# The odd layer's key and value weights at the end of the first expert stage, and routed rows read and added in quarters of a tile

## The chip, the cores and the metric

The kernel runs on one core of a Trainium2 chip. The metric is the device time of one execution in microseconds. The core has TensorE (PE: matrix products, with PEld its weight loads), VectorE (DVE), ScalarE (ACT), GpSimd (POOL) and SyncE (SP), which here only issues DMAs and clears semaphores. Engines run their own instruction lists and wait on semaphores. Sixteen DMA engines are shared by all queues; DMAs from SyncE go through one hardware queue, those of GpSimd through a software queue.

## The reference

A two-layer backbone over 256 context tokens and 256 latent tokens, width 1024, all in float32. Layer 0 mixes with neighbourhood and grouped-query attention, layer 1 with differential attention. Behind each mixer comes a mixture of experts: 64 experts of width 256, each token goes to 8 of them. What matters here is the step between the two layers:

```python
y = moe_ffn(tokens, *moe_args)            # layer 0, 512 tokens: sum over 8 routed experts + shared expert
xc = xc + g_fc * y[:, :L]                 # context
x = x + g_f * y[:, L:]                    # latent
...
h = modulate(rms_norm(x, norm_mix[l]), sh_m, sc_m)      # layer 1
q, k, v = jnp.split(hs @ w_in, 3, axis=-1)              # diff_mixer: w_in is 1024 x 3072
```

## The kernel before, in words

Tokens lie in four tiles of 128 rows: tiles 0 and 1 the context, 2 and 3 the latents. The program is a sequence of stages; at the end of each, all engines meet in a block end, then SyncE clears the stage's semaphores one by one (L245), then all meet again.

Stage `ffn0` (`feed_forward`) computes the routed experts in R rounds of 128 slots. In a round, GpSimd gathers token rows (L1355), TensorE transposes them (L1418), multiplies by gate and up weights (L1448), ScalarE and VectorE form the hidden rows (L1456, L1462), TensorE transposes them (L1470) and multiplies by the down weights (L1492), VectorE and ScalarE scale the result by the token's gate (L1529, L1538), and GpSimd scatters it to `y_rows` in HBM (L1363). `y_rows` holds, for each token, its 8 expert rows. Gate and up weights of an expert take one of four slots of `wb` (`wgu`, two 1 MB halves each), the down weights one of five other slots, two of them in `hT`. SyncE loads them in the order of the experts and waits, before it fills a slot, until TensorE has used it for the last time. After the last scatter GpSimd waits for both scatter semaphores (L1721). Then `further` reads a counter that says whether an expert got more rows than planned; only in that case does a slow fallback run (`fb_sp` and others). It isn't taken with these inputs.

The same four slots of `wb` also serve `Stream`, a list of weight blocks of 512 columns (2 MB) which SyncE feeds with `core.stream.feed` and TensorE takes with `core.stream.take`. Block n goes to slot n % 4. The first four blocks of the odd layer's projection, `diff_w_kv`, hold the keys' and values' columns; their first block has number 31 and goes to slot 3.

Stage `mix1` (`combine_project`) reads the eight rows of each token back, adds them up, gates the sum and adds it to the residual `x`, takes the norm, transposes, modulates, and projects to keys, values and (for the latents) queries. SyncE reads the rows of a tile in two halves of four rows (L2054). VectorE waits for a half and adds (L2104 to L2109), multiplies with the gate (L2111), adds to `x` (L2112). ScalarE squares and sums (L2150) and takes the root (L2153), VectorE inverts and scales (L2114 to L2118), TensorE transposes (L2075), VectorE and ScalarE modulate half of the transposed tile each (L2123, L2159), and TensorE multiplies (L2092): 4 blocks for each of 4 tiles, then 2 query blocks for tiles 2 and 3, 40 products of 8 matmuls. TensorE transposes tile t+1 ahead of the last block of tile t.

Of the kernel before, what the change touches and what calls it, by code (L numbers as in the profile page):

```python
# [16 lines left out]
ALU = mybir.AluOpType  # L17
ACT = mybir.ActivationFunctionType
AX = mybir.AxisListType.X

P = 128
D = 1024
# [14 lines left out]
E = 64  # L37
TOP_K = 8
F = D // 4
# [4 lines left out]
TILES = (CTX + LAT) // P  # L44
# [218 lines left out]
STREAM = 4  # L263
# [869 lines left out]
def feed_forward(core, r, sw, final_norm):  # L1133
# [15 lines left out]
    last = r.out is not None  # L1149
    XS = RING - 1 if last else RING  # L1150
    with Stage(nc, f"ffn{layer}") as st:
# [45 lines left out]
        if last:  # L1197
# [3 lines left out]
            gain = core.pool[:, 3, D:2 * D]  # L1201
# [8 lines left out]
        r.slots = wgu  # L1210
        wd = [core.pool[:, 0, :], core.pool[:, 1, :], core.hT[:, 0:4, :].rearrange("p k t -> p (k t)"),
# [369 lines left out]
        def fb_sp(sp, b, e, n):  # L1581
            sp.wait_ge(fb_free, n + 1)
            for dst, src in ((wgu[0][:, 0, :], r.gate_src), (wgu[0][:, 1, :], r.up_src), (wd[0], r.down_src)):
                sp.dma_start(dst, r.of(src, e)).then_inc(fb_w_in, 16)
# [62 lines left out]
        def fb_pe(pe, b, e, n):  # L1647
# [11 lines left out]
            w = wgu[0].rearrange("p i (k f) -> p k i f", f=F)  # L1659
# [23 lines left out]
        with nc.Block() as block:  # L1683
            @block.sync
            def _(sp):
# [8 lines left out]
                for q in range(E - LAG, E):  # L1694
                    sp_down(sp, q)
                if last:
                    sp.wait_ge(xb_turned, R)
                    sp.dma_start(gain, final_norm.rearrange("(o d) -> o d", o=1).to_broadcast([P, D])).then_inc(gain_in, 16)
# [315 lines left out]
def combine_project(core, r, w):  # L2014


    nc = core.nc
    COLS = BLOCK
    HALF = TOP_K // 2
    first = core.stream.start["diff_w_kv"]  # L2020
    kv = 2 * D // COLS
    with Stage(nc, "mix1") as st:
        yr = st.sb("yr", [P, 2, HALF, D])
# [3 lines left out]
        y_in = [st.sem("y_in0"), st.sem("y_in1")]  # L2027
# [19 lines left out]
        with nc.Block() as block:  # L2047
            @block.sync
            def _(sp):
                def rows(n):  # L2050
                    if n >= 2:

                        sp.wait_ge(y_used, n - 1)
                    sp.dma_start(yr[:, n % 2], y_view[n // 2][:, HALF * (n % 2):HALF * (n % 2 + 1), :]).then_inc(y_in[n % 2], 16)  # L2054

                rows(0)
                rows(1)
                core.stream.feed(sp, first + 1, first)
                rows(2)
                core.stream.feed(sp, first + 2, first)  # L2060
                rows(3)
                core.stream.feed(sp, first + kv, first)
                for n in range(4, 2 * TILES):
                    rows(n)
                core.stream.feed(sp, core.stream.end["diff_w_out"], first, lambda b: (summed, last_use(b)))
# [31 lines left out]
            def _(dve):  # L2097
                link = Chain(dve, own)
                for t in range(TILES):
                    acc = xn[:, t, :]  # L2100
                    for half in range(2):
                        dve.wait_ge(y_in[half], 16 * (t + 1))
                        v = yr[:, half]
                        link(nc.vector.tensor_tensor(v[:, 0:2], v[:, 0:2], v[:, 2:4], ALU.add))  # L2104
                        if half == 0:
                            nc.vector.tensor_tensor(acc, v[:, 0], v[:, 1], ALU.add).then_inc(y_used, 1)
                        else:
                            link(nc.vector.tensor_tensor(acc, acc, v[:, 0], ALU.add))
                            nc.vector.tensor_tensor(acc, acc, v[:, 1], ALU.add).then_inc(y_used, 1)  # L2109
                        dve.wait_ge(y_used, 2 * t + half + 1)  # L2110
                    link(nc.vector.tensor_tensor(acc, acc, grow[:, t // 2, :], ALU.mult))  # L2111
# [35 lines left out]
            def _(act):  # L2147
# [13 lines left out]

                square(0)
# [325 lines left out]
```

## Time and profile before

| what | value |
|---|---|
| three runs | 1970.25, 1970.87, 1976.96 us; median 1970.87 |
| profiled execution | 1975.1 us, span 1973.3 us |
| TensorE busy | 1739.5 us, 88% of the span |
| VectorE, ScalarE, GpSimd busy | 568.7, 312.3, 207.1 us |
| DMA | 560.50 MB, mean 284 GB/s over the span |
| mean granted TensorE clock | 0.956 |

A profile is one execution. Busy times are those of the engines' instructions; waits are read between them. A clock of 1.0 is the upper of TensorE's two levels (2.4 GHz), 0.50 the lower (1.2 GHz). The span is not made of one limit: in the expert stages the weights stream at about 390 GB/s and TensorE is nearly full, in the stages between, short chains over all engines count.

### The profile page before, as it was taken

Reading aid. Unit: us, or ns where it says so; the run is one execution under the profiler, and the core shown is the slowest. Engines: PE = TensorE matmul, PEld = TensorE weight load, DVE = VectorE, ACT = ScalarE, POOL = GpSimd, SP = SyncE. Lnnn points to the kernel's source line nnn. Section 1 sums busy time; section 2 is a strip of 40 time slices with the busy share of each in tenths; the row PEclk is TensorE's granted clock in tenths of the full one; section 3 lists DMA queues with packets and bytes.
Section 4 is the critical chain, followed back from the end, with each engine's and each line's share of the span. In section 5 each row is a group of like instructions: output and inputs, shape, how many; then the busy total and the mean of one; then the engine's idle time right before and its main releaser. Section 6 shows DMA issues by size and latency. Waiting matters only on the chain. (4 is left out here: it accounts for less than half of the span.)

```text
span 1973.3 us, 23640 instructions
## 1 busy us (share of the span) xinstructions
PE 1739.5 (88%) x8663; PEld 793.9 (40%) x8663; DVE 568.7 (29%) x1345; ACT 312.3 (16%) x686; POOL 207.1 (10%) x197
## 2 busy tenths in 40 slices
PE   4999999998999999999998199888779989988895
PEld 2544544446443334333433044354423333333231
DVE  2131445435422222212221343275321111111112
ACT  2102333212011111111111011062201011001011
POOL 0300222100111111111111000020010000000000
PEclk8999999997999999999999599989889999999998
DMA  9414667005699999999997570400499999999992
GB/s 355 120 64 143 229 225 243 14 0 192 269 418 399 409 419 395 416 418 402 418 412 321 228 287 25 146 5 0 158 420 407 407 420 396 420 419 419 419 406 98
DMA packets 125188, 560.50 MB, mean 284 GB/s; under 512 B 17266, under 2 KB 22785, under 8 KB 74896
## 3 DMA queue, kind: packets, MB, share of 16 engines
q1 hardware_dynamic: 106960, 512.20, 65.0%
q0 software_dynamic: 17248, 43.62, 5.8%
q10 hardware_dynamic: 864, 3.15, 0.4%
q8 instruction: 71, 1.16, 0.2%
q14 instruction: 45, 0.37, 0.1%
HBM read 549.94 MB, written 26.80 MB: 292 GB/s over the span
## 5 line engine op out<-in xcount | busy, mean ns | idle before, releaser
L1448 PE MATMUL ps<-wb,pool 128*32 128x512 f32 (+2 forms) x2608 | 486.7, 600 | 19.3 <-issue 19.3
L1448 PEld LDWEIGHTS ps<-wb,pool 128*32 128x32 f32 (+2 forms) x2608 | 159.8, 124 | 306.6 <-issue 306.5
L1462 DVE TENSOR_TENSOR ffn_hid<-ffn_sg,ps 128x256 f32<-128x256 f32 x71 | 29.9, 422 | 607.9 <-ACT ffn_sg L1456 607.9
L1492 PE MATMUL ps<-pool,ffn_hidT 128*32 128x512 f32 (+2 forms) x584 | 165.9, 604 | 23.9 <-DVE ffn_hidT L1477 10.8
L1492 PE MATMUL ps<-hT,ffn_hidT 128*32 128x512 f32 (+2 forms) x680 | 157.7, 599 | 19.7 <-DVE ffn_hidT L1477 14.8
L1355 POOL DMA_INDIRECT pool<-h_rows,ffn_index x71 | 74.6, 1051 | 655.9 <-PE ps L1418 306.5
L2092 PE MATMUL ps<-wb,hT 128*128 128x512 f32 x320 | 140.8, 602 | 1.6 <-issue 1.6
L1456 ACT ACTIVATE ffn_sg<-ps 128x256 f32<-128x256 f32 x71 | 27.2, 383 | 489.1 <-PE ps L1448 489.1
L1492 PE MATMUL ps<-sh_wd,ffn_hidT 128*32 128x512 f32 (+2 forms) x272 | 100.3, 597 | 4.6 <-DVE ffn_hidT L1477 2.6
L1418 PEld LDWEIGHTS ps<-const,pool 128*128 128x128 f32 x568 | 77.5, 194 | 66.6 <-issue 63.3
L1510 PE MATMUL ps<-x_res,rw 128*128 128x512 f32 x224 | 103.1, 603 | 0.9 <-ACT x_res L1538 0.9
L1418 PE MATMUL ps<-const,pool 128*128 128x128 f32 x568 | 94.1, 289 | 8.3 <-DMA pool<-h_rows,ffn_index 6.2
L1363 POOL DMA_INDIRECT y_rows<-sh_wgu,ffn_index x43 | 43.1, 1002 | 486.5 <-ACT sh_wgu L1538 472.0
L2092 PEld LDWEIGHTS ps<-wb,hT 128*128 128x128 f32 x320 | 61.6, 194 | 78.2 <-issue 78.2
L1433 ACT COPY pool<-ps 128x512 f32<-128x512 f32 x71 | 41.6, 585 | 296.5 <-PE ps L1418 296.5
L985 PE MATMUL ps<-wb,hT 128*128 128x512 f32 x192 | 83.4, 593 | 3.4 <-PEq L241 3.4
L1448 PE MATMUL ps<-ffn_wgu_more,pool 128*32 128x512 f32 (+1 forms) x208 | 73.9, 622 | 5.7 <-issue 5.7
L948 POOL TENSOR_SCALAR attn_pn<-attn_p,attn_mx 128x256 f32<-128x256 f32 (+1 forms) x43 | 53.1, 1235 | 241.3 <-DVE attn_mx L886 239.7
L1426 DVE COPY pool<-ps 128x512 f32<-128x512 f32 x71 | 48.8, 688 | 90.3 <-PE ps L1418 89.9
L1448 PE MATMUL ps<-sh_wgu,pool 128*32 128x512 f32 (+2 forms) x256 | 72.7, 602 | 1.6 <-issue 1.6
L368 PE MATMUL ps<-wb,silu 128*32 128x512 f32 x384 | 54.1, 687 | 22.1 <-DMA wb<-in_ada_w_dram 17.6
L1492 PEld LDWEIGHTS ps<-pool,ffn_hidT 128*32 128x32 f32 (+2 forms) x584 | 45.3, 127 | 69.4 <-issue 62.6
(287 smaller groups left out, 1905.0 us busy)
## 6 DMA issues: line engine op xcount, KB each, us to landing
wb<-in_expert_w_gate_dram SPq DMA_DIRECT2D x108, 1024.0 KB, 12.9
wb<-in_expert_w_up_dram SPq DMA_DIRECT2D x108, 1024.0 KB, 17.8
pool<-in_expert_w_down_dram SPq DMA_DIRECT2D x52, 1024.0 KB, 18.8
hT<-in_expert_w_down_dram SPq DMA_DIRECT2D x52, 1024.0 KB, 17.1
wb<-in_ada_w_dram SPq DMA_DIRECT2D x24, 2048.0 KB, 9.6
sh_wd<-in_expert_w_down_dram SPq DMA_DIRECT2D x24, 1024.0 KB, 19.8
mix_yr<-y_rows SPq DMA_DIRECT2D x8, 2048.0 KB, 11.8
wb<-in_diff_w_in_dram SPq DMA_DIRECT2D x6, 2048.0 KB, 16.8
```

The source lines that it names most:

```text
L368: mm = nc.tensor.matmul(core.ps[g:g + 32, bank, :], core.silu[:, k, :], w[:, k, :], start=k < 4, stop=k >= 4, skip_group_check=True, tile_ ...
L948: nc.gpsimd.tensor_scalar(pn[:, n % 4, 0:nk], p[:, n % 4, 0:nk], mx[:, n % 4, 3:4], None, ALU.mult).then_inc(norm_pool, 1)
L985: mm = nc.tensor.matmul(core.ps[:, n % 6, :], core.hT[:, k, oT_at(t)], wo[:, k, :], start=k == 0, stop=k == KD - 1)
L1355: pool.indirect_dma_start(out=xs[:, s, :], out_offset=None, in_=r.h_rows, in_offset=bass.IndirectOffsetOnAxis(ap=index[:, n, 0:1], axis=0) ...
L1363: pool.indirect_dma_start(out=r.y_rows, out_offset=bass.IndirectOffsetOnAxis(ap=index[:, n, 1:2], axis=0), in_=y[:, n % 2, :], in_offset=N ...
L1418: mm = nc.tensor.transpose(core.ps[:, x_bank(half), (k % 4) * P:(k % 4 + 1) * P], xs[:, s, k:D:KD], core.c("ident"))
L1426: nc.vector.tensor_copy(xT[:, n % 2, 0:4, :].rearrange("p k c -> p (k c)"), core.ps[:, x_bank(0), :]).then_inc(xa_ready, 1)
L1433: nc.scalar.copy(xT[:, n % 2, 4:8, :].rearrange("p k c -> p (k c)"), core.ps[:, x_bank(1), :]).then_inc(xb_ready, 1)
L1448: mm = nc.tensor.matmul(core.ps[lo:lo + width, gu_bank(n), :], xT[:, n % 2, k, lo:lo + width], w[:, k], start=k == 0, stop=k == KD - 1, sk ...
L1492: mm = nc.tensor.matmul(core.ps[lo:lo + width, down_bank(half), :], hidT[:, n % 2, k, lo:lo + width], wd_at(q % DR, half, k), start=k == 0 ...
L1510: mm = nc.tensor.matmul(core.ps[:, 4 + 2 * i + half, :], back_hot[:, n % 2, i * P:(i + 1) * P], y[:, n % 2, half * 512:(half + 1) * 512], ...
L2092: mm = nc.tensor.matmul(core.ps[:, n % 6, :], core.hT[:, k, t * P:(t + 1) * P], wb[:, k, :], start=k == 0, stop=k == KD - 1)
```

## The change

It has five parts.

1. At the end of SyncE's list in `ffn0`, ahead of `further`, the four key and value blocks are fed. Each waits until the last expert that uses its slot has been multiplied. They are no longer fed in `mix1`.
2. The fallback's gate and up weights go to `hT` instead of slot 0 of `wb`, which now holds a key and value block.
3. `mix1` reads a tile in four quarters of two rows: 16 DMAs of 1 MB instead of 8 of 2 MB, with a semaphore and a buffer for each quarter.
4. VectorE adds quarter by quarter. The first three are summed, gated and added to `x`; the last is summed, gated and added to `x` by itself.
5. ScalarE takes one square root of a constant ahead of everything in `mix1`.

```diff
     XS = RING - 1 if last else RING
+    ahead = core.stream.start["diff_w_kv"]
...
+        fb_wgu = core.hT[:].rearrange("p k t -> p (k t)").rearrange("p (i n) -> p i n", i=2)
...
                 for q in range(E - LAG, E):
                     sp_down(sp, q)
+                if not last:
+                    for n in range(ahead, ahead + STREAM):
+
+                        user = max(q for q in range(E) if q % GU == n % STREAM)
+                        sp.wait_ge(gu_ready, plan.last(user) + 1)
+                        core.stream.feed(sp, n + 1, ahead)
...
-                rows(0)
-                rows(1)
-                core.stream.feed(sp, first + 1, first)
...
+                for n in range(PARTS * TILES):
+                    if n >= PARTS:
+
+                        sp.wait_ge(y_used, n - PARTS + 1)
+                    i = n % PARTS
+                    sp.dma_start(yr[:, i], y_view[n // PARTS][:, PART * i:PART * (i + 1), :]).then_inc(y_in[i], 16)
...
-                        if half == 0:
+                    gain = grow[:, t // 2, :]
+                    for i in range(PARTS):
+                        dve.wait_ge(y_in[i], 16 * (t + 1))
+                        v = yr[:, i]
+                        if i == 0:
                             nc.vector.tensor_tensor(acc, v[:, 0], v[:, 1], ALU.add).then_inc(y_used, 1)
+                        elif i < PARTS - 1:
+                            link(nc.vector.tensor_tensor(v[:, 0], v[:, 0], v[:, 1], ALU.add))
+                            nc.vector.tensor_tensor(acc, acc, v[:, 0], ALU.add).then_inc(y_used, 1)
                         else:
...
+                            link(nc.vector.tensor_tensor(acc, acc, gain, ALU.mult))
+                            link(nc.vector.tensor_tensor(core.x[:, t, :], core.x[:, t, :], acc, ALU.add))
+                            link(nc.vector.tensor_tensor(v[:, 0], v[:, 0], v[:, 1], ALU.add))
+                            nc.vector.tensor_tensor(acc, v[:, 0], gain, ALU.mult).then_inc(y_used, 1)
+                        dve.wait_ge(y_used, PARTS * t + i + 1)
                     nc.vector.tensor_tensor(core.x[:, t, :], core.x[:, t, :], acc, ALU.add).then_inc(x_ready, 1)
...
+                nc.scalar.activation(rs[:, 1, 0:1], core.c("ones")[:, 0:1], ACT.Sqrt)
                 square(0)
```

How the instructions stand. On SyncE at the end of `ffn0`, before (L1129, L1130, L1347 load the last expert's weights, L1555 is the read of the counter in `further`):

```order
L1129 DMA wb<-in_expert_w_gate_dram 128x2048
L1130 DMA wb<-in_expert_w_up_dram 128x2048
L1122 TENSOR_LOAD ffn_eid
L1122 ISA x2
L1347 ISA
L1347 DMA hT<-in_expert_w_down_dram 128x2048
L1555 TENSOR_LOAD ffn_longest
L1555 ISA x2
```

and after:

```order
L1129 DMA wb<-in_expert_w_gate_dram 128x2048
L1130 DMA wb<-in_expert_w_up_dram 128x2048
L1122 TENSOR_LOAD ffn_eid
L1122 ISA x2
L1349 ISA
L1349 DMA hT<-in_expert_w_down_dram 128x2048
L295 DMA wb<-in_diff_w_in_dram 128x8x512 x4
L1557 TENSOR_LOAD ffn_longest
L1557 ISA x2
```

The four blocks now stand between the last expert's down weights and the read of the counter. In `mix1`, SyncE before:

```order
L2054 DMA mix_yr<-y_rows 128x4096 x2
L295 DMA wb<-in_diff_w_in_dram 128x8x512
L2054 DMA mix_yr<-y_rows 128x4096
L295 DMA wb<-in_diff_w_in_dram 128x8x512
L2054 DMA mix_yr<-y_rows 128x4096
L295 DMA wb<-in_diff_w_in_dram 128x8x512 x2
L2054 DMA mix_yr<-y_rows 128x4096 x4
L295 DMA wb<-in_diff_w_in_dram 128x8x512 x2
```

and after (with the clears of `ffn0` ahead of it):

```order
L245 ISA x73
L241 UNCONDITIONAL_BRANCH
L2057 UNCONDITIONAL_BRANCH
L2064 DMA mix_yr<-y_rows 128x2048 x16
L295 DMA wb<-in_diff_w_in_dram 128x8x512 x2
L295 DMA wb<-in_diff_w_out_dram 128x8x512 x2
```

Only rows are left ahead of the two query blocks. On VectorE, one tile of `mix1` before:

```order
L2104 TENSOR_TENSOR mix_yr<-mix_yr 128x2048
L2106 TENSOR_TENSOR mix_xn<-mix_yr 128x1024
L2104 TENSOR_TENSOR mix_yr<-mix_yr 128x2048
L2108 TENSOR_TENSOR mix_xn<-mix_xn,mix_yr 128x1024
L2109 TENSOR_TENSOR mix_xn<-mix_xn,mix_yr 128x1024
L2111 TENSOR_TENSOR mix_xn<-mix_xn,ffn_gate 128x1024
L2112 TENSOR_TENSOR x_res<-x_res,mix_xn 128x1024
```

and after (the line numbers are those of the changed file; the wait for the last quarter is on L2111):

```order
L2106 TENSOR_TENSOR mix_xn<-mix_yr 128x1024
L2108 TENSOR_TENSOR mix_yr<-mix_yr 128x1024
L2109 TENSOR_TENSOR mix_xn<-mix_xn,mix_yr 128x1024
L2108 TENSOR_TENSOR mix_yr<-mix_yr 128x1024
L2109 TENSOR_TENSOR mix_xn<-mix_xn,mix_yr 128x1024
L2111 TENSOR_TENSOR mix_xn<-mix_xn,ffn_gate 128x1024
L2112 TENSOR_TENSOR x_res<-x_res,mix_xn 128x1024
L2113 TENSOR_TENSOR mix_yr<-mix_yr 128x1024
L2114 TENSOR_TENSOR mix_xn<-mix_yr,ffn_gate 128x1024
L2116 TENSOR_TENSOR x_res<-x_res,mix_xn 128x1024
```

Seven instructions, two of them twice as wide, have become ten; behind the last wait for rows stand five of 1024 elements where one of 2048 and four of 1024 stood.

## Rows read from the trace of the kernel before

**Rows 1.** The page's first line: span of the profiled execution, and its instructions.

```profile
span 1973.3 us, 23640 instructions
```

**Rows 2.** Windows: us, busy us of each engine (instructions), PEclk, DMA share, GB/s.

```profile
1095.00:1101.50 6.50, 0.00 (x0) 0.00 (x0) 0.00 (x0) 0.00 (x0) 0.00 (x0) 0.50 0.00 0
...
1106.40:1133.50 27.10, 1.97 (x8) 1.59 (x9) 14.22 (x15) 4.14 (x8) 0.00 (x0) 0.50 0.98 387
1133.50:1157.80 24.30, 24.29 (x56) 11.11 (x57) 10.83 (x11) 3.11 (x6) 0.00 (x0) 0.89 1.03 412
1157.80:1276.50 118.70, 118.66 (x290) 53.21 (x288) 40.61 (x54) 14.62 (x31) 0.00 (x0) 1.00 0.30 111
```

**Rows 3.** Timeline: start us, us, engine, line, operation, tiles, [idle before <-releaser].

```profile
1082.99 0.38 ACT L1456 ACTIVATE ffn_sg<-ps 128x256 f32<-128x256 f32 x1 [8.73 <-PE ps L1448]
...
1090.58 0.97 POOL L1363 DMA_INDIRECT y_rows<-sh_wgu,ffn_index  x1 [14.57 <-issue]
...
1106.37 0.82 SPq L2054 DMA_DIRECT2D mix_yr<-y_rows  x2
```

**Rows 4.** L1683 and L245 from 1090 to 1110 us: durations in ns, first and last start.

```profile
L1683 POOLq DRAIN  x1: 7079/7079/7079, 1094.3 to 1094.3; - x1
...
L245 SPq EVENT_SEMAPHORE_RANGE_CLEAR  x73: 25/25/49, 1101.7 to 1106.1; - x73
```

**Rows 5.** Timeline of tile 0 of the stage `mix1`, from the first rows to TensorE.

```profile
1113.84 2.29 DVE L2104 TENSOR_TENSOR mix_yr<-mix_yr 128x2048 f32<-128x2048 f32 x1 [26.01 <-DMA mix_yr<-y_rows]
...
1118.84 2.29 DVE L2104 TENSOR_TENSOR mix_yr<-mix_yr 128x2048 f32<-128x2048 f32 x1 [1.44 <-DMA mix_yr<-y_rows]
1121.16 1.22 DVE L2108 TENSOR_TENSOR mix_xn<-mix_xn,mix_yr 128x1024 f32<-128x1024 f32 x1
...
1124.94 1.22 DVE L2112 TENSOR_TENSOR x_res<-x_res,mix_xn 128x1024 f32<-128x1024 f32 x1
...
1127.36 1.28 ACT L2153 ACT_TABLE_LOAD   x1
1127.38 0.15 DVE L2114 TENSOR_SCALAR mix_rs<-mix_ss 128x1 f32<-128x1 f32 x1 [1.22 <-ACT mix_xn L2150]
1128.65 0.20 ACT L2153 ACTIVATE mix_rs<-mix_rs 128x1 f32<-128x1 f32 x1
...
1129.90 1.97 PE L2075 MATMUL ps<-const,mix_xn 128*128 128x128 f32 x8 [41.14 <-DVE mix_xn L2118]
...
1133.51 23.59 PE L2092 MATMUL ps<-wb,hT 128*128 128x512 f32 x48 [1.64 <-issue]
```

**Rows 6.** Timeline of the same two small steps in tile 1.

```profile
1148.00 0.15 DVE L2114 TENSOR_SCALAR mix_rs<-mix_ss 128x1 f32<-128x1 f32 x1 [1.22 <-ACT mix_xn L2150]
...
1148.19 0.20 ACT L2153 ACTIVATE mix_rs<-mix_rs 128x1 f32<-128x1 f32 x1 [0.22 <-DVE mix_rs L2114]
```

**Rows 7.** Scatters of L1363, issue to landing in us: at 1062.4, at 1090.6, all 43.

```profile
DMA to landing us min/median/max: 9.2/9.2/9.2
...
DMA to landing us min/median/max: 2.6/2.6/2.6
...
DMA to landing us min/median/max: 2.6/8.6/9.6
```

**Rows 8.** Hardware queue from 1062 to 1073 us: packets, MB, share of 16 engines.

```profile
q1 hardware_dynamic: 579, 4.22, 92.0%
```

**Rows 9.** L295: ns of the first four issues; landing of the four, of the first.

```profile
L295 SPq DMA_DIRECT2D wb<-in_diff_w_in_dram x4: 427/1272/6786, 1107.2 to 1126.3; - x4
...
DMA to landing us min/median/max: 16.6/18.7/25.1
...
wb<-in_diff_w_in_dram SPq DMA_DIRECT2D x1, 2048.0 KB, 16.9
```

**Rows 10.** Timeline: rows of tile 2 ready, and the transposes of tile 2.

```profile
1174.03 0.75 DVE L2118 TENSOR_SCALAR mix_xn<-x_res,mix_rs 128x1024 f32<-128x1024 f32 x1
...
1185.28 1.04 PE L2075 MATMUL ps<-const,mix_xn 128*128 128x128 f32 x8
```

More of the change, by code:

```diff
@@ L1582, in fb_sp @@
             sp.wait_ge(fb_free, n + 1)
-            for dst, src in ((wgu[0][:, 0, :], r.gate_src), (wgu[0][:, 1, :], r.up_src), (wd[0], r.down_src)):
+            for dst, src in ((fb_wgu[:, 0, :], r.gate_src), (fb_wgu[:, 1, :], r.up_src), (wd[0], r.down_src)):
                 sp.dma_start(dst, r.of(src, e)).then_inc(fb_w_in, 16)
@@ L1658, in fb_pe @@
             pe.wait_ge(fb_w_in, 48 * n + 48)
-            w = wgu[0].rearrange("p i (k f) -> p k i f", f=F)
+            w = fb_wgu.rearrange("p i (k f) -> p k i f", f=F)
             for k in range(KD):
@@ L2018, in combine_project @@
     COLS = BLOCK
-    HALF = TOP_K // 2
+    PART = 2
+    PARTS = TOP_K // PART
     first = core.stream.start["diff_w_kv"]
@@ L2022, in combine_project @@
     with Stage(nc, "mix1") as st:
-        yr = st.sb("yr", [P, 2, HALF, D])
+        yr = st.sb("yr", [P, PARTS, PART, D])
         grow = r.ffn_gate
         ss, rs = st.sb("ss", [P, TILES]), st.sb("rs", [P, 3, TILES])
-        y_in = [st.sem("y_in0"), st.sem("y_in1")]
+        y_in = [st.sem(f"y_in{i}") for i in range(PARTS)]
         y_used, x_ready, own = st.sem("y_used"), st.sem("x_ready"), st.sem("own")
@@ L2049, in _ @@
             def _(sp):
[L2050 to L2054, printed above, removed]
-                rows(0)
-                rows(1)
-                core.stream.feed(sp, first + 1, first)
[L2059 to L2064, printed above, removed]
+                for n in range(PARTS * TILES):
[3 more added lines that the diff above has]
+                    sp.dma_start(yr[:, i], y_view[n // PARTS][:, PART * i:PART * (i + 1), :]).then_inc(y_in[i], 16)
                 core.stream.feed(sp, core.stream.end["diff_w_out"], first, lambda b: (summed, last_use(b)))
@@ L2100, in _ @@
                     acc = xn[:, t, :]
[L2101 to L2104, printed above, removed]
-                        if half == 0:
+                    gain = grow[:, t // 2, :]
[3 more added lines that the diff above has]
+                        if i == 0:
                             nc.vector.tensor_tensor(acc, v[:, 0], v[:, 1], ALU.add).then_inc(y_used, 1)
-                        else:
[L2108 to L2111, printed above, removed]
+                        elif i < PARTS - 1:
+                            link(nc.vector.tensor_tensor(v[:, 0], v[:, 0], v[:, 1], ALU.add))
+                            nc.vector.tensor_tensor(acc, acc, v[:, 0], ALU.add).then_inc(y_used, 1)
+                        else:
+                            link(nc.vector.tensor_tensor(acc, acc, gain, ALU.mult))
[3 more added lines that the diff above has]
+                        dve.wait_ge(y_used, PARTS * t + i + 1)
                     nc.vector.tensor_tensor(core.x[:, t, :], core.x[:, t, :], acc, ALU.add).then_inc(x_ready, 1)
```

## The prediction, made before the changed kernel ran

> **What bounds the kernel now.** I read the page, then a table of windows around the boundary between the first expert stage (`ffn0`) and the stage that the change touches (`mix1`), then the timeline there, then waits and landings. The profiled execution took 1975.1 us, its span is 1973.3 us [rows 1], and 1.8 us lie around it; the median of the runs is 1970.87 us, 4.2 us below it. The sum is made on the profiled execution and its difference is then taken from the median. From 1133.5 to 1276.5 us TensorE has no hole (24.29 busy of 24.30 us, 118.66 of 118.70) [rows 2]: once `mix1` projects, TensorE bounds it, and no weight block is late. Before that it stands still, from the end of the last down projection to 1129.9 us. So the change can win or lose only in that pause, and what counts is when the first projection begins, 1133.51 us [rows 5].
>
> The pause is one chain. The gate-up product of the last round ends at about 1082.98 (ScalarE starts on it at 1082.99); the last scatter of expert rows is issued at 1090.58 [rows 3] and lands 2.6 us later [rows 7]. GpSimd then leaves the stage through a DRAIN of 7.08 us that begins at 1094.3, and SyncE clears 73 semaphores from 1101.7 to 1106.1 [rows 4]. The first rows are asked for at 1106.37 [rows 3]. The second half of tile 0 is there at 1118.84, 12.47 us later; VectorE needs until 1126.2 to sum and gate it, then come the norm, TensorE's transposes at 1129.90 and the first product at 1133.51 [rows 5]. From 1095 to 1101.5 the DMA engines move nothing, and from 1106.4 on 387 GB/s [rows 2].
>
> **The change, part by part.**
>
> *Weights moved ahead.* Four 2 MB blocks (8.39 MB) now stand at the end of SyncE's list in `ffn0`. The first goes into slot 3, which the last expert uses, so nothing is issued before 1082.98. At 387 GB/s the four take 21.7 us. A 2 MB read of rows lands its 2.10 MB 7.47 us after the issue [rows 3, 5]; 5.4 of these are transfer at that rate, so about 2.1 us are start. The weights are thus done near 1083.0 + 2.1 + 21.7 = 1106.8, and the first rows would begin to arrive only 2.1 us after their issue at 1106.37 or later: no overlap. What is gained by the earlier weights alone is nothing. Block 0 was issued at 1107.24 and landed 16.9 us later [rows 9], at 1124.1, 9.4 us ahead of its first use; rows of tile 0 stand ahead of it in the same queue, so they did not wait for it. The work that hid these loads is VectorE's sum; if that cover were gone, block 0 would still be in time.
>
> Its cost is on the last scatter. That scatter now runs beside 8.39 MB of weights. Alone it lands in 2.6 us; the one issued at 1062.4 beside expert weights took 9.2, and over all 43 the median is 8.6 and the maximum 9.6 [rows 7]. GpSimd waits for this landing, the DRAIN comes after it, SyncE's clears after that, so every microsecond is paid in full. No row shows this scatter beside these blocks, so I bound it: 0 from its own landing alone, +7.0 from the maximum (9.6 - 2.6). Between them I go by packet length. Beside the expert weights the hardware queue moved 4.22 MB in 579 packets [rows 8], 7.3 KB each; a key and value block is 8 x 512 floats a partition, 2 KB pieces. If the delay of 6.6 us (9.2 - 2.6) shrinks with the length of the packet that a scatter's packet must let pass, it is 6.6 x 2.0/7.3 = **+1.8 us**, and this value I take.
>
> The Trainium skill (DMA: Bandwidth & Descriptors, Queues, rings and completion order) speaks against it: a DMA engine takes turns between queues by whole packets of some 9 to 17 descriptors. By that a turn of the weights would be 18 to 34 KB, no less than beside the experts, and the delay would be the whole +6.6. No row here decides it; it is the rival below.
>
> SyncE's four issues: one issue of such a block took between 0.43 and 6.8 us [rows 9], the long ones while earlier blocks were still queued. Two short and two long are 14.5 us from 1083.0, so SyncE reaches the end of the stage near 1097.5, before GpSimd's DRAIN ends at 1101.4 (1094.3 + 7.08) [rows 4]. Cost 0; behind those issues stands only SyncE's branch and barrier. If all four took 6.8 it would be there at 1110.2, 8.8 us late.
>
> *Rows in quarters.* 16 DMAs of 1 MB for 8 of 2 MB, in the same order on the same queue; four reads with nothing between them bring the same 4.19 MB, so the last quarter lands 12.47 us after the first issue, as the second half did. After the landing of the second half VectorE ran one 2048-wide add (2.32 us with the gap: 1118.84 to 1121.16) and four 1024-wide operations, the last of them started at 1124.94 (1.26 us each: (1124.94 - 1121.16)/3) [rows 5], 7.36 us. Now the wait for the last quarter stands before the gating product, so five 1024-wide operations follow it: 5 x 1.26 = 6.30. The third quarter lands some 2.6 us before the last, and its two adds take 2.52, so they are just done. **-1.06 us**. Bounds: -1.1, and 0 if the smaller pieces cost the last quarter a microsecond. Over a tile VectorE's work grows from 10.9 (2 x 2.32 + 5 x 1.26) to 12.6 us. For tiles 1 to 3 that lies under TensorE: rows of tile 2 were ready at 1174.8 and the transposes ran at 1185.28, 10.5 us later [rows 10]. Cost 0, and still 0 if the cover shrank by 8 us. The rows of tiles 1 to 3 wait on VectorE's use of the same quarter one tile before; the weights no longer share the queue with them. Nothing there is late.
>
> *Square root ahead.* The table load (1.28 us at 1127.36) moves to the stage's beginning, where ScalarE idles some 20 us. VectorE's step ends at 1127.53 and the root begins at 1128.65, 1.12 us [rows 5]; in tile 1, without a load, 1148.15 to 1148.19, 0.04 us [rows 6]. **-1.08 us**, bounds -1.3 and 0 (if another load followed).
>
> The Trainium skill (ScalarE: Activation LUTs, What ACT_TABLE_LOAD costs) puts a load with its drain at 2.66 us. Here the root starts 0.01 us after the load's end [rows 5], so the drain isn't in this gap and the row decides; by the page the term would be about -2.5 and the sum -1.6.
>
> *Small things.* Two more semaphores are cleared at the end of `mix1`: 2 x 0.06 us (4.4 us over 73) [rows 4], **+0.12**. The fallback's gate and up weights go to `hT` instead of slot 0; the fallback is a branch that this input doesn't take, no row shows it. TensorE's clock: granted 0.50 from 1095 to 1133.5 and 0.89 over the next 24.3 us [rows 2], so at half speed for some 5.3 us after it resumes. The pause and the work around it keep their shape, term 0; a rise that comes 3 us earlier or later against the work moves 1.5 us.
>
> **Sum.** +1.8 - 1.06 - 1.08 + 0.12 = -0.2 us: 1974.9 on the profiled execution, 1970.7 as a median.
>
> **Rivals.**
> 1. *The scatter waits its full time* (slower). Delay 6.6 instead of 1.8: sum +4.6, 1975.5 us. For it: all loaded scatters of the trace [rows 7], and GpSimd's place on the chain. Against: the packets beside it are 2 KB. It makes the kernel slower than before as soon as the landing takes over 4.6 us (2.6 + 2.0), the point where it has eaten the two gains.
> 2. *The scatter isn't delayed, or the clock rises early* (faster). Delay 0: -2.0, 1968.9; with the clock 3 us early -3.5, 1967.4. For it: the scatter is the smallest kind. Against: 21.7 us of transfers lie over its whole life.
> 3. *SyncE or the transfers become the bound.* Four long issues: +8.8 - 2.0, 1977.7; or the last block, issued near 1097.5, needs 16.6 us as the quickest of the four before did [rows 9]: it ends at 1114.1 and the rows, due to begin at 1110.3 (1106.37 + 1.8 + 2.1), come 3.8 us late: +3.6, 1974.5.
> 4. *The change doesn't do what it says*: slot 3 comes first and its user is the last expert, so "ahead" means only the pause. That is in the sum already. Were the loads held back until the scatter has landed at 1093.2 (as if the two could not run together), they would end at 1117.0 (1093.2 + 2.1 + 21.7), rows due at 1108.5 would be 8.5 late, and the sum 8.5 - 2.0 = +6.5, 1977.4.
>
> **How the numbers follow.** Forecast (within 2 us of nothing) 0.50; rival 1 0.24; rival 2 0.14; rival 3 0.08; rival 4 0.04. The runs before spread from 1970.25 to 1976.96, so a median may be off by some 2 us by itself. 8 in 10: from rival 2 with that scatter, 1966.5, to rival 1 and most of rival 3, 1977.5. About 0.5% (9.85 us) is what a measurement of this kernel can tell from no change. No case but a sum of several reaches it: the whole chain from 1106.37 to 1133.51 is 27.1 us, of which 12.47 is the arrival of rows that nothing shortens. Slower by more needs a landing like the worst with long issues on top, 0.05; faster by more 0.03; within it 0.92.
>
> **What would show it.** In the profile after: four issues of the weights at about 1083; the last scatter's landing, 4.4 us if the packet argument holds, 9 if rival 1 does; a DRAIN near 7.1 us; the first rows asked for near 1108.2; 6.3 us from the last quarter's arrival to the end of the sum; the root some 0.05 us after its input; TensorE's first product about 25.0 us after the first issue of rows, and no hole behind it. I am wrong if TensorE stops inside `mix1`, if the DRAIN grows, or if the time between that first product and the end of the program changes by more than 1 us.

## The result, and the profile after

The changed kernel takes 1978.85 us (median of 19 runs, 1975.49 to 1985.27); the kernel before, run beside it, takes 1971.89 us (19 runs, 1965.19 to 1980.43). The ratio is 1.0035 with a 95% interval of [1.0022, 1.0047]: slower by 7 us (4.3 to 9.3). Single runs of the two kernels overlap, but the interval excludes no change; the difference is below the 0.5% that the prediction set as its bound. The forecast was 1970.7 us, that is no change; 1978.85 is 1.35 us above the upper end of the range. Of the 8.2 us between forecast and result 1.0 is the starting point: the prediction took the median of three runs, 1970.87, where 19 give 1971.89.

The profiled execution of the changed kernel is its slowest of the 19, 1985.27 us, and that of the kernel before 1975.1 us. So the two traces differ by 10.2 us where the medians differ by 7, and the trace may be used for terms that are the same in every kernel, but not its total. The page's first line, to be read against [rows 1]:

```profile
span 1983.5 us, 23671 instructions
```

The pause before `mix1`, in the timeline after (start us, us, engine, line, operation, tiles, idle before and releaser), to be read against [rows 3, 5]:

```profile
1084.69 11.71 SPq L295 DMA_DIRECT2D wb<-in_diff_w_in_dram  x4
1084.70 0.38 ACT L1458 ACTIVATE ffn_sg<-ps 128x256 f32<-128x256 f32 x1 [8.63 <-PE ps L1450]
...
1092.29 0.97 POOL L1365 DMA_INDIRECT y_rows<-sh_wgu,ffn_index  x1 [14.46 <-issue]
1112.53 25.39 SPq L2064 DMA_DIRECT2D mix_yr<-y_rows  x9
1112.54 1.28 ACT L2166 ACT_TABLE_LOAD   x1 [21.34 <-PEq L241]
...
1117.42 1.23 DVE L2106 TENSOR_TENSOR mix_xn<-mix_yr 128x1024 f32<-128x1024 f32 x1 [27.88 <-DMA mix_yr<-y_rows]
1119.98 1.22 DVE L2108 TENSOR_TENSOR mix_yr<-mix_yr 128x1024 f32<-128x1024 f32 x1 [1.33 <-DMA mix_yr<-y_rows]
...
1125.01 1.22 DVE L2111 TENSOR_TENSOR mix_xn<-mix_xn,ffn_gate 128x1024 f32<-128x1024 f32 x1
...
1130.05 1.23 DVE L2116 TENSOR_TENSOR x_res<-x_res,mix_xn 128x1024 f32<-128x1024 f32 x1
...
1132.49 0.15 DVE L2118 TENSOR_SCALAR mix_rs<-mix_ss 128x1 f32<-128x1 f32 x1 [1.22 <-ACT mix_xn L2154]
1132.67 0.20 ACT L2157 ACTIVATE mix_rs<-mix_rs 128x1 f32<-128x1 f32 x1 [0.22 <-DVE mix_rs L2118]
...
1133.92 1.97 PE L2075 MATMUL ps<-const,mix_xn 128*128 128x128 f32 x8 [43.44 <-DVE mix_xn L2122]
...
1137.53 2.90 PE L2092 MATMUL ps<-wb,hT 128*128 128x512 f32 x3 [1.65 <-issue]
```

Read it from both ends. From the end of the gate-up product to the scatter's issue it is 7.59 us in both traces (1084.70 to 1092.29; 1082.99 to 1090.58). From the scatter's issue to the first rows it is 20.24 us and was 15.79: +4.45. From the first rows to TensorE's first product it is 25.00 us and was 27.14: -2.14. After its second quarter, at 1119.98, VectorE has no idle time until the sum ends at 1131.28, nine operations of 1.26 us.

Where the +4.45 is. The scatter's landing in us, from the view of its line:

```profile
DMA to landing us min/median/max: 6.9/6.9/6.9
```

and by line, durations in ns and first and last start: SyncE and GpSimd as they leave the stage, the clears of its semaphores, and the four issues of the weights:

```profile
L1685 SPq DRAIN  x1: 7/7/7, 1097.2 to 1097.2; - x1
L1685 POOLq DRAIN  x1: 7079/7079/7079, 1100.3 to 1100.3; - x1
...
L245 SPq EVENT_SEMAPHORE_RANGE_CLEAR  x73: 25/30/49, 1107.6 to 1112.2; - x73
...
L295 SPq DMA_DIRECT2D wb<-in_diff_w_in_dram x4: 389/2226/6737, 1084.7 to 1089.7; - x4
```

To the hundredth, the landing went from 2.64 to 6.91 us (+4.27), the DRAIN is 7.079 us to the nanosecond as before [rows 4], and begins 1.1 us after the landing in both. From the first of the 73 clears to the first rows it is 4.88 us instead of 4.71: the median clear now takes 30 ns where it took 25. SyncE was at the end of the stage at 1097.2, ten microseconds before GpSimd, so its issues cost nothing.

What the scatter ran beside, from 1092.3 to 1099.3 (queue: packets, MB, share of 16 engines):

```profile
q1 hardware_dynamic: 1257, 2.54, 97.2%
q0 software_dynamic: 144, 0.18, 7.2%
```

The weights do go in pieces of 2.0 KB (2.54 MB in 1257 packets; 7.3 KB in [rows 8]). The windows of the same stretches as in [rows 2] (us, busy us of each engine, PEclk, DMA share, GB/s):

```profile
1112.50:1137.50 25.00, 1.97 (x8) 1.57 (x8) 15.74 (x18) 4.35 (x9) 0.00 (x0) 0.50 0.83 336
1137.50:1161.80 24.30, 24.27 (x59) 11.27 (x60) 13.47 (x18) 3.97 (x9) 0.00 (x0) 0.93 0.48 173
1161.80:1279.00 117.20, 117.20 (x286) 52.57 (x284) 42.62 (x56) 13.77 (x29) 0.00 (x0) 1.00 0.30 108
```

TensorE again has no hole from its first product on. The granted clock in the first 24.3 us is 0.93, was 0.89: it rose 3.3 us after the first product instead of 5.5 us. From the first product to the first clear `mix1` took 1.1 us less (146.9 against 148.0).

Behind `mix1` no instruction was changed, and yet the time from there to the end of the program grew from 691.79 to 699.02 us. Four windows of the kernel before: turning queries and keys, the output projection of the odd layer, the second expert stage, the end of the last stage with its clears:

```profile
1282.50:1292.41 9.91, 6.99 (x48) 6.78 (x48) 6.25 (x19) 5.95 (x14) 0.00 (x0) 0.83 0.08 21
1355.87:1390.34 34.47, 31.52 (x96) 15.74 (x96) 12.04 (x31) 3.72 (x7) 0.00 (x0) 1.00 0.00 0
1399.80:1968.41 568.61, 487.27 (x2872) 196.38 (x2872) 110.04 (x278) 56.72 (x102) 30.91 (x28) 0.96 0.92 378
1968.41:1973.24 4.83, 0.00 (x0) 0.00 (x0) 0.00 (x0) 0.00 (x0) 0.00 (x0) 0.50 0.01 2
```

and of the changed one:

```profile
1285.59:1296.53 10.94, 8.03 (x48) 7.82 (x48) 6.25 (x19) 5.95 (x14) 0.00 (x0) 0.75 0.07 18
1360.37:1397.65 37.28, 34.32 (x96) 16.82 (x96) 12.04 (x31) 3.72 (x7) 0.00 (x0) 0.92 0.00 0
1406.65:1977.91 571.26, 488.27 (x2872) 196.41 (x2872) 110.12 (x278) 56.78 (x102) 30.91 (x28) 0.96 0.92 377
1977.91:1983.41 5.50, 0.00 (x0) 0.00 (x0) 0.00 (x0) 0.00 (x0) 0.00 (x0) 0.50 0.00 0
```

The same 48 transposes cost 1.03 us more at a granted clock of 0.75 instead of 0.83, the same 96 products 2.81 us more at 0.92 instead of 1.00 (VectorE's and ScalarE's busy times are the same to 0.01 us), the second expert stage 2.65 us more. The last line is no clock: SyncE clears the same 84 semaphores there, and the stretch is 5.50 instead of 4.83 us. Only part of that is the clears: from the first to the last of them it is 4.82 instead of 4.57, and from the last to the end of the span 0.68 instead of 0.25. Summed over all stages, first to last clear, it is 16.63 instead of 15.39 us. The two differences make +1.67 (1.24 + 0.43), called "clears" below. Of the 1.24, 0.11 are the two additional semaphores, 0.46 is longer pauses among the 14 clears behind the output projection (1.20 instead of 0.74 us), and the rest is clears of 30 instead of 25 ns.

The 10.2 us of the two traces are thus: +4.27 scatter, -2.14 rows and root, +1.67 clears, -1.1 clock in `mix1`, +6.5 in the three stages behind it, and +1.0 in stages that are the same (the first, `adaln`, was 1.69 us longer). The experiments ask which of these belong to the change and which to the draw of one execution.

### The profile page after: what moved, and what is told of

The parts are those of the page before. It is cut to its first block and busy times, and to the rows that moved or that the text cites. A ratio compares the mean times of both kernels' runs of the same rounds, so it can differ in the third digit from the quotient of the medians.

```text
span 1983.5 us, 23671 instructions
## 1 busy us (share of the span) xinstructions
PE 1744.6 (88%) x8663; PEld 796.5 (40%) x8663; DVE 575.1 (29%) x1357; ACT 313.0 (16%) x687; POOL 206.8 (10%) x197
## 5 line engine op out<-in xcount | busy, mean ns | idle before, releaser
L1450 PE MATMUL ps<-wb,pool 128*32 128x512 f32 (+2 forms) x2608 | 489.3, 602 | 20.1 <-issue 20.1
L1494 PE MATMUL ps<-pool,ffn_hidT 128*32 128x512 f32 (+2 forms) x584 | 164.8, 598 | 23.6 <-DVE ffn_hidT L1479 10.8
```

The source lines that it names most:

```text
L1450: mm = nc.tensor.matmul(core.ps[lo:lo + width, gu_bank(n), :], xT[:, n % 2, k, lo:lo + width], w[:, k], start=k == 0, stop=k == KD - 1, sk ...
L1494: mm = nc.tensor.matmul(core.ps[lo:lo + width, down_bank(half), :], hidT[:, n % 2, k, lo:lo + width], wd_at(q % DR, half, k), start=k == 0 ...
```

## Experiments

Two theories at first. *The scatter*: the landing beside the weights is the loss, and without it the two gains are left. *The clock*: the loss is the granted clock behind `mix1`, and depends on when the pause ends. In what was expected of the runs these are theories A and D; B says only that part of the loss sits behind `mix1`, C, E and G put it down to the code of the program, F to the number of semaphores, and `turn1` is the stage that turns queries and keys. The kernel before was timed again on each chip; its median was 1974.26 (35 runs) beside the first four kernels, 1975.26 (35) beside the next four, 1973.92 (29) beside the last four. Kernels are compared with the one beside them only.

### The changed kernel with no weights ahead

```diff
-                    for n in range(ahead, ahead + STREAM):
...
-                        core.stream.feed(sp, n + 1, ahead)
...
+    FEED = {3: 1, 5: 2, 7: 4}
+                    if n in FEED:
+                        core.stream.feed(sp, first + FEED[n], first)
```

> The changed kernel without its first part: the four key and value blocks are fed in mix1 between the rows, as before; rows in quarters and the early square root stay. Theory A (the whole cost is the last scatter, which lands 4.3 us later beside the weights, and the rows and the root give 2.1 back): 2.1 us faster than before, the scatter lands in 2.6 us, 25.0 us from the first issue of rows to the first product. Theory B (some 5 us of the loss sit behind mix1, in the length of VectorE's and SyncE's lists or in TensorE's clock there, and come with the quarters): 3 to 5 us slower than before, though the first product comes 2.1 us earlier.

Measured: 1976.19 us, ratio 1.0015 [0.9997, 1.0032]. The scatter lands in 2.64 us again, the first product comes 25.04 us after the first rows. So the scatter's loss comes with the loads and goes with them. But the kernel is not 2 us faster than the one before, as the scatter's theory had it: the end of the last stage stays at 5.50 us, and the stages behind `mix1` take as long as in the changed kernel (window of the projection):

```profile
1354.65:1392.08 37.43, 34.47 (x96) 16.81 (x96) 12.04 (x31) 3.72 (x7) 0.00 (x0) 0.92 0.00 0
```

### The kernel before with only the weights ahead

The loop of the change goes into the kernel before (with the fallback's weights in `hT`, which it needs); rows in halves, root late.

> The kernel before with the first part of the change alone (blocks at the end of ffn0, fallback weights in hT); rows in halves, no early root. Theory A: 4.3 us slower than before; the scatter lands in about 6.9 us, the DRAIN stays 7.08, rows are asked for 4.4 us later, then 27.1 us to the first product. Theory B in its other form (the residual comes with the early weights): 8 to 10 us slower, with 4.4 of them in front of mix1 and the rest behind it.

Measured: 1979.75 us, ratio 1.0032 [1.0009, 1.0055]. Its timeline around the scatter:

```profile
1085.08 11.80 SPq L295 DMA_DIRECT2D wb<-in_diff_w_in_dram  x4
1092.67 0.97 POOL L1365 DMA_INDIRECT y_rows<-sh_wgu,ffn_index  x1 [16.19 <-issue]
...
1112.81 0.83 SPq L2062 DMA_DIRECT2D mix_yr<-y_rows  x2
```

and the scatter's landing:

```profile
DMA to landing us min/median/max: 7.0/7.0/7.0
```

Issue to landing 7.0, issue to rows 20.1 us, rows to first product 27.0 as before; turning 9.92 and projection 34.47 us as before. This is the scatter's term alone, +4.3, and it is slower. The earlier weights give nothing back.

### The changed kernel with one block ahead

`range(ahead, ahead + 1)`, the other three fed between the rows (`FEED = {5: 2, 7: 4}`).

> The changed kernel, but only the first of the four blocks is fed at the end of ffn0; the other three come in mix1 between the rows. One block is 2 MB, 5.4 us at 387 GB/s, so it is over at about 1090.5, when the last scatter is only issued. Theory A: the scatter lands in 2.6 to 3.0 us, and the kernel is 2.1 us faster than before (1.7 to 2.1). If what hurts is not sharing the DMA engines but a DMA issued ahead of the branch in itself: 2 us slower or more.

Measured: 1975.17 us, ratio 1.0013 [0.9992, 1.0034]. The scatter and the first rows in its timeline:

```profile
1086.83 0.97 POOL L1365 DMA_INDIRECT y_rows<-sh_wgu,ffn_index  x1 [14.48 <-issue]
...
1102.79 10.22 SPq L2065 DMA_DIRECT2D mix_yr<-y_rows  x6
```

and the landings, of the block ahead (issued at 1079.2) and of the scatter:

```profile
DMA to landing us min/median/max: 9.1/9.1/9.1
...
DMA to landing us min/median/max: 2.6/2.6/2.6
```

The block has landed at 1088.3, 1.5 us after the scatter's issue and before its landing at 1089.5, and the scatter is undisturbed: what costs the scatter time is the load that still stands in the queues behind that. That the total is not 2 us faster is no effect of the early DMA either: the kernel with none ahead stands as far above its sum.

### The kernel before with the fallback's weights in `hT`

> The kernel before, with only the fallback's gate and up weights in hT instead of slot 0, code that isn't executed. Both theories: no difference (within 2 us). Its spread also shows what the same program does from run to run; a difference of 4 us or more would say that the layout of the code counts (theory C).

Measured: 1972.30 us, ratio 0.9997 [0.9977, 1.0018]; the three stages behind `mix1` as before (9.90, 34.47 and 568.92 us). No cost of this edit is seen.

### A shift of the end of `mix1`

The next three take the clock's side. Useless operations at the end of VectorE's list in `mix1` let the stage end later and change nothing else: two adds of 1.26 us in the kernel without weights ahead, one copy of 0.8 us in the kernel before, three such copies (2.4 us) in the changed one.

```diff
+                for _ in range(2):
+                    link(nc.vector.tensor_tensor(yr[:, 3, 0], yr[:, 3, 0], yr[:, 3, 1], ALU.add))
```

> [...] Theory D (clock steps): turn1 goes back from 11.1 to 9.9 us and the odd output projection from 37.4 to 34.5 us, so that the later kernel is 1 to 3 us faster than e1_no_ahead, about 0 to 1 us slower than before. Theory E (the code of the quarters makes the later stages longer): both stages stay at 11.1 and 37.4, and the kernel is 2.5 us slower than e1_no_ahead.

Measured: 1972.89 us, ratio 0.9992 [0.9973, 1.0011]. Turning and projection, in windows:

```profile
1278.68:1288.49 9.81, 6.91 (x48) 6.70 (x48) 6.25 (x19) 5.96 (x14) 0.00 (x0) 0.84 0.08 20
1351.96:1386.43 34.47, 31.51 (x96) 15.73 (x96) 12.03 (x31) 3.72 (x7) 0.00 (x0) 1.00 0.00 0
```

> [...] Theory D: turn1 grows from 9.9 to about 11.1 us and the odd output projection from 34.5 to 37.4, the kernel is 4 to 6 us slower than before for an operation of 0.8 us. Theory E: both stages stay, 0.8 us slower.

Measured: 1977.79 us, ratio 1.0022 [1.0004, 1.0040]:

```profile
1280.00:1290.62 10.62, 7.70 (x48) 7.49 (x48) 6.24 (x19) 5.95 (x14) 0.00 (x0) 0.78 0.07 19
1353.90:1391.28 37.38, 34.42 (x96) 16.81 (x96) 12.03 (x31) 3.72 (x7) 0.00 (x0) 0.92 0.00 0
```

> [...] Theory D: turn1 9.9 to 10.2 us, output projection about 34.5, the kernel 1 to 3 us faster than the changed kernel (3 to 5 us slower than before). Theory E: 2.4 us slower than the changed kernel.

Measured: 1980.37 us, ratio 1.0032 [1.0016, 1.0049]; turning 10.07, projection 34.47 us, scatter 6.9 us.

The kernel with 2.5 us of useless work is not slower than the one without it, but 1972.62 against 1976.68 us in the mean, and it is 1.9 us below the kernel before beside it where the other is 3.3 above. The one with 0.8 us more work is 4 us slower (0.8 to 7.9). In the trace it is the same 96 products that take 34.47 or 37.4 us, by the clock granted at their beginning. All three stage patterns came as the clock's theory had them, but each is one execution. Theory E falls for these two stages: two of the three kernels have the code of the quarters and the short pattern. In the changed kernel the 2.4 us gave back the projection's 2.8 us, but the total is 6.3 us above the kernel before (3.2 to 9.7) where that of the changed kernel is 6.9. The 1 to 3 us that the theory gave it are neither seen nor excluded. The trace with the 0.8 us also bears less than it seems to: its clock rose 3.1 us after the first product where the kernel before has 5.5, long before the added operation ran, so the long pattern there can't be put down to the operation alone.

### One block ahead, and one gate

The third kernel, with the last quarter added before the gating: nine operations a tile instead of ten.

```diff
-                            link(nc.vector.tensor_tensor(acc, acc, gain, ALU.mult))
-                            link(nc.vector.tensor_tensor(core.x[:, t, :], core.x[:, t, :], acc, ALU.add))
-                            nc.vector.tensor_tensor(acc, v[:, 0], gain, ALU.mult).then_inc(y_used, 1)
+                            link(nc.vector.tensor_tensor(acc, acc, v[:, 0], ALU.add))
+                            nc.vector.tensor_tensor(acc, acc, gain, ALU.mult).then_inc(y_used, 1)
```

> Kernel e3_one_ahead (only the first block early, so the last scatter is alone) with the gate applied once: the last quarter is added to the sum of the others, then gate and residual, 9 operations a tile in place of 10 and 4 behind the last wait. From the first issue of rows to the first product 23.7 us (25.0 less 1.26), the scatter 2.7 us. [...] Theory E (ten operations, two more semaphores): like e3_one_ahead less 1.3.

Measured: 1974.53 us, ratio 1.0000 [0.9983, 1.0017]. The first product comes 23.83 us after the first rows, 1.2 less: four operations follow the last wait for rows instead of five, so the one that is saved is saved in full. The total decides nothing between the theories.

### Two unused semaphores, and the root alone

> The kernel before with two more semaphores in mix1 that nobody uses. In all kernels with quarters the clears take longer everywhere, also in stages before the changed code (18 clears of the first stage 1.29 us instead of 1.24, the last stage 5.50 instead of 4.83; 1.67 us over the program). Theory F (the number of semaphores or the length of SyncE's list does it): the clears take 1.67 us more here too, mix1 0.1, and the kernel is 1.7 us slower than before. Theory G (it comes with the code of the quarters): the clears stay at 1.24 and 4.83, and the kernel is 0.1 us slower.

Measured: 1974.02 us, ratio 0.9993 [0.9973, 1.0014]. The clears of the whole program, by line:

```profile
L245 SPq EVENT_SEMAPHORE_RANGE_CLEAR  x281: 25/25/49, 42.3 to 1973.4; - x141
```

281 clears as in the changed kernel, at the old 25 ns (changed kernel: 30 ns in the middle of 281). Two more semaphores cost 0.11 us, in `mix1`, as the prediction had it; the longer clears are not theirs. The trace showed something else. The pause is the old one (27.13 us to the first product), and still the clock rose 3.4 us after it instead of 5.5, and turning took 10.99 and the projection 37.38 us. So the longer pattern can fall to a kernel whose timing is that of before: at least in part it is drawn per execution. The window of its projection:

```profile
1353.15:1390.53 37.38, 34.41 (x96) 16.81 (x96) 12.03 (x31) 3.72 (x7) 0.00 (x0) 0.92 0.00 0
```

The kernel before with the early root alone:

```diff
+                nc.scalar.activation(rs[:, 1, 0:1], core.c("ones")[:, 0:1], ACT.Sqrt)
```

> The kernel before with only the early square root. Both theories: from the first issue of rows to the first product 27.1 - 1.08 = 26.0 us. [...] Without clock steps it is 1.1 us faster.

Measured: 1973.54 us, ratio 0.9988 [0.9970, 1.0005]; the first product 25.92 us after the first rows, -1.2 us. Its trace has the long pattern too, 11.03 us of turning and this projection:

```profile
1351.74:1389.14 37.40, 34.44 (x96) 16.78 (x96) 12.04 (x31) 3.72 (x7) 0.00 (x0) 0.92 0.00 0
```

Neither of the two kernels is measurably slower than the one before. The pattern in the one profiled execution doesn't tell what the median does.

### Larger pieces beside the scatter

In the kernel with only the weights ahead, eight 1 MB tiles of expert weights in 8 KB pieces are loaded instead, for nothing; key and value blocks come in `mix1`. One run.

> The kernel of e2_only_ahead, but what is loaded at the end of ffn0 are eight 1 MB tiles of expert weights in 8 KB pieces (useless, the same 8.39 MB into the same slots), and the key and value blocks come in mix1 as before. Packet-length argument of the prediction: the last scatter lands later than beside 2 KB pieces (7.0 us), about 9.2. If the delay doesn't depend on the length of the pieces: 7.0 us again.

The scatter's landing, and the queues while it runs, from 1087.6 to 1096.2 (packets, MB, share of 16 engines):

```profile
DMA to landing us min/median/max: 8.6/8.6/8.6
```

```profile
q1 hardware_dynamic: 453, 3.32, 95.0%
q0 software_dynamic: 144, 0.18, 5.7%
```

Measured: 1979.52 us. The landing takes 8.57 us, a delay of 5.9 beside packets of 7.3 KB (3.32 MB in 453); in the changed kernel it is 4.3 beside 2.0 KB. It is the same scatter at the same place, 144 packets and 0.18 MB in both. Shorter pieces do help, but much less than in proportion. A straight line through the two would be 3.6 us plus 0.31 us for each KB; it is an estimate, since two points can't show that the dependence is a line. Clears are longer here too (30 ns in the middle of 281), though rows come in halves. Only the landing is read from this kernel: SyncE waits there for the useless loads too, and reaches the end of the stage 0.5 us after GpSimd.

### One block ahead, one gate, fifteen semaphores

The kernel with one gate, with two semaphores merged into others, so that `mix1` has fifteen of them, as in the kernel before.

> e8_one_ahead_one_gate with two semaphores less (VectorE's two towards TensorE made one, that of the queries replaced by the stage's own chain), so that mix1 has 15 as before. Theory F: clears as in the kernel before, 1.7 us less than e8; total 1.7 us faster than e8, 1 to 5 us faster than before. Theory G: clears as in e8, no difference to it. mix1 171.6 us in both.

Measured: 1970.35 us (1962.58 to 1974.97), ratio 0.9975 [0.9953, 0.9996], the only one whose interval lies below 1, by 0.04%. Clears of the program by line, and windows of turning, projection and the last clears:

```profile
L245 SPq EVENT_SEMAPHORE_RANGE_CLEAR  x279: 25/29/49, 42.9 to 1965.3; - x140
...
1274.75:1284.63 9.88, 6.97 (x48) 6.76 (x48) 6.24 (x19) 5.96 (x14) 0.00 (x0) 0.83 0.08 20
1348.12:1382.59 34.47, 31.52 (x96) 15.73 (x96) 12.03 (x31) 3.71 (x7) 0.00 (x0) 1.00 0.00 0
...
1960.44:1965.54 5.10, 0.00 (x0) 0.00 (x0) 0.00 (x0) 0.00 (x0) 0.00 (x0) 0.50 0.00 0
```

The first product comes 23.6 us after the first rows. The clears are as many as in the kernel before and still longer: 5.10 us at the end against 4.83, +1.1 over the program. Their number is not the cause, and theory F, the number of semaphores, falls.

### All of them together

What the terms measured in the pause and in the clears give, beside the whole (ratio times the kernel before), in us:

| kernel | scatter | rows, root, added work | clears | sum | measured (95%) |
|---|---|---|---|---|---|
| changed | +4.3 | -2.1 | +1.7 | +3.9 | +6.9 (4.3 to 9.3) |
| no weights ahead | 0 | -2.1 | +1.7 | -0.4 | +3.0 (-0.6 to 6.3) |
| only weights ahead | +4.3 | 0 | 0 | +4.3 | +6.3 (1.8 to 10.9) |
| one block ahead | 0 | -2.2 | +1.7 | -0.5 | +2.6 (-1.6 to 6.7) |
| fallback only | 0 | 0 | 0 | 0 | -0.6 (-4.5 to 3.6) |
| no weights ahead, 2.5 us later | 0 | +0.4 | +1.7 | +2.1 | -1.6 (-5.3 to 2.2) |
| before, 0.8 us later | 0 | +0.8 | 0 | +0.8 | +4.3 (0.8 to 7.9) |
| changed, 2.4 us later | +4.3 | +0.3 | +1.7 | +6.3 | +6.3 (3.2 to 9.7) |
| one block, one gate | 0 | -3.3 | +1.7 | -1.6 | 0.0 (-3.4 to 3.4) |
| two semaphores | 0 | 0 | +0.1 | +0.1 | -1.4 (-5.3 to 2.8) |
| root only | 0 | -1.2 | 0 | -1.2 | -2.4 (-5.9 to 1.0) |
| one gate, 15 semaphores | 0 | -3.5 | +1.1 | -2.4 | -4.9 (-9.3 to -0.8) |

The kernel with 8 KB pieces ran once and is left out. The sum lies within the interval in all but the changed kernel, whose +3.9 is just below its own (with 0.8 us of added work it stands at the edge). What is left over runs from -3.7 to +3.5 us, the size of what the clock moves in the windows above. The intervals are as wide, so the table can't test the terms one by one; these are read from the traces.

## Why the prediction was wrong, point by point

**The bound and the chain: right.** The change acts only on the pause. The weights ahead gained nothing (the kernel with only them is slower by its whole scatter term), and TensorE had no hole behind its first product. Scatter, landing, DRAIN of 7.08 us, clears, rows: each microsecond of the landing came out at the rows' issue (4.27 of landing and 0.17 of clears make the +4.45).

**The scatter: the step that failed.** "If the delay shrinks with the length of the packet" it is +1.8 us; it is +4.3 (6.91 - 2.64), and 5.9 beside packets of 7.3 KB. I scaled the whole delay with the piece's length, where by the two points most of it, some 3.6 us if the dependence is a line, did not depend on it. Nor was it the full 6.6 of rival 1, whose direction and point of decision (a landing over 4.6 us) came true: the truth lay halfway. By the rule that I weighed (the Trainium skill, DMA: Bandwidth & Descriptors, Queues, rings and completion order: turns by whole packets of some 9 to 17 descriptors) I had put the delay at no less than beside the experts; beside 2 KB pieces it is a third smaller (4.3 against 6.6), so that reading falls too. Nor did it follow from the rule: counted in the same way, a turn beside the experts' 7.3 KB packets [rows 8] would be 66 to 124 KB, an estimate from that page's figure, so the rule as well asks for a delay in proportion to the piece. What the fixed part is made of stays open, and with it whether the scatter waits at the DMA engines, at memory or at both.

**Issues: right.** Predicted: SyncE at the end of the stage near 1097.5, two short issues and two long, 14.5 us. Measured: 1097.2, the four from 0.39 to 6.74 us, 11.7 in all. That the two times agree to 0.3 us is partly luck: the issues were 2.8 us shorter, and this execution came to them 1.7 us later. Rivals 3 and 4 fall: the last block landed at 1110.5, 2.0 us before the rows were asked for, and the transfers ran while the scatter did (391 GB/s from 1092.3 to 1099.3).

**Quarters and root: right.** Predicted 25.0 us from first rows to first product; measured 25.00 in the changed kernel and 25.04 and 24.94 in two others. The root alone gave -1.2 (said: -1.08), and starts 0.03 us after its input ends (1132.64 to 1132.67; said: 0.05). The page's figure for the table load (the Trainium skill, ScalarE: Activation LUTs, What ACT_TABLE_LOAD costs: 2.66 us) would have made it -2.5 by the prediction's estimate; the row decided rightly. The quarters' share is -0.9 (said: -1.06), with 6.3 us from 1125.01 to the sum's end. The last quarter, issued at 1113.87, landed 10.98 us later at 1124.85, and VectorE's adds of the third ended at 1124.97: they were "just done", as forecast. With five operations behind that wait, one gate fewer saved another 1.2 us.

**Small things: the second failure.** The two semaphores cost the +0.12 that was forecast (0.11 in the kernel that has only them). But in the changed kernel nearly every second clear takes 30 ns instead of 25, in stages that no edit touches, and pauses among and behind them are longer: +1.67 us in all, a term that the sum had at 0.12. The cause is open. It is not the number of semaphores (281 at 25 ns in one kernel, 279 at 29 in another), nor quarters (30 ns with halves in one kernel). Where SyncE's code lies for each stage was not tried.

**The clock: term 0 was wrong, and its bound of 1.5 us too narrow.** I allowed for a rise earlier or later inside `mix1`, and it came 2.2 us earlier, worth 1.1 us. I did not allow for the stages behind: turning and projection together have cost 44.3 to 48.5 us for the same instructions, and the second expert stage 568.6 to 571.3. "I am wrong if the time between that first product and the end changes by more than 1 us" came true: 839.8 before (1973.3 - 1133.5), 846.0 after (1983.5 - 1137.5), +6.2.

Is this share the change's? The traces show what the pattern goes with: how long after the clock's rise `mix1` ends. From that rise to the stage's first clear it is 142.4 to 142.5 us in four kernels (before, only weights ahead, fallback only, fifteen semaphores) and 145.4 and 145.9 in the two with 2.4 and 2.5 us of added work. These six have the projection of 34.47 us. In the six whose projection takes 37.3 to 37.5 us (changed, no weights ahead, one block ahead, before with 0.8 us, two semaphores, root only) it is 143.3 to 144.4. The other two, at 142.7 and 143.8, have 36.3 and 36.0 us. But when the clock rises is partly a draw: it came 5.5 us after the first product in the kernel before, and 3.4 and 3.1 us after it in the two kernels that have the same instructions up to there (two semaphores, 0.8 us later).

It is not a draw alone. The mean granted clock was read for each run, and a run whose clock is 0.001 lower is some 1.2 us longer (an estimate from the 99 runs of the kernel before, chip by chip). Without weights ahead the mean over 12 runs is 0.9542 (standard error 0.0007), beside it the kernel before has 0.9572 (0.0005): by that estimate 3.6 us, all that this kernel is above the one before. The changed kernel has 0.9551 over its 19 runs (0.0005), the kernel before 0.9562 to 0.9577 on the three other chips; some of that is the longer pause itself, which runs at half clock. So what is left over goes with a lower clock in the mean of many runs, and what lowers it isn't shown.

Shown is +3.9 us out of +6.9: scatter, rows and root, clears. I don't claim the other 3 us for a mechanism.

## What to carry to other kernels

A load put into an idle stretch is not free when a small transfer on the chain that ends the stretch runs beside it: price that transfer beside the load, and if no row shows it, take the loaded rows and not a scaling that only an argument supports. Ahead of such a transfer put only what is done before it moves (here one block of four), and ask first whether the load was late at all. A change of 2 us in a program whose granted clock moves stages by 3 us without any edit has to be read from the stage it acts on; the whole tells it only after many runs, and a harmless edit elsewhere can look as large.

## What the runs showed of the hardware

- GpSimd's DRAIN after its last scatter took 7.079 us in the traces of all fourteen kernels, whether the scatter before it landed in 2.6, 7 or 8.6 us.
- A scatter of 0.18 MB in 144 packets landed in 2.6 us alone, in 6.9 to 7.0 beside loads in 2 KB pieces (three traces), in 8.6 beside packets of 7.3 KB (one trace).
- The same 96 products cost 34.47 us when the clock is granted in full and 37.4 when they begin at half of it (0.92 in the mean), and which it is went with how long after the clock's rise the stage `mix1` had ended, and changed without any edit ahead of it.
- The end of the last stage, with the same 84 semaphores to clear, cost 4.83, 5.10 or 5.50 us by the program, with no semaphore, order or wait changed there. The clears themselves took 4.57 us in the first and 4.82 in the other two; the rest lies around them.
